# Where the tiles lie in on-chip memory: the order of the regions reversed in a two-block transformer kernel

## The chip, the cores and the metric

The kernel runs on one core of one Trainium2 chip. The metric is the time of one execution on the device, in microseconds. Before the change it was 2476.69 us, the median of 3 runs (2471.95 to 2477.06).

A core has TensorE (PE in the profile), which multiplies: it holds a 128x128 *stationary* operand and streams a *moving* operand of up to 512 columns past it, and the result goes to one of 8 banks of PSUM. VectorE (DVE), ScalarE (ACT) and GpSimd (POOL) work on tiles elementwise; SyncE (SP) issues the transfers from HBM. The on-chip memory (SBUF) has 128 partitions; a tile takes the same range of bytes in each, and "address" below means the first byte of a tile in a partition.

## The reference, cut to what matters

A sequence of 512 tokens of width 1024 goes through two blocks (the lines above the loop, and the loop), all in float32:

```
x = x + 0.5 * rms_norm(swiglu_ffn(rms_norm(x)))            # up0, down0: 1024 -> 2*2816 -> 1024
x = x + rms_norm(token_mixer(rms_norm(x)))                 # mixin, hgrn2 and mLSTM, mixout
x = x + 0.5 * rms_norm(swiglu_ffn(rms_norm(x)))            # up1, down1
for layer in range(2):
    mix = mixer_ab(x) if layer == 0 else mixer_c(x)        # ab, about; cin, cout
    x = layer_norm(alpha * x + mix)
    x = layer_norm(alpha * x + cross_attend(x, mem))       # kv, q, wo; mem has 256 rows
    x = layer_norm(alpha * x + conv_ffn(x))                # up2, down2; up3, down3
```

Most of the arithmetic is products of activations with weight matrices. Each such product is done in three matmuls: a float32 matrix W is split into W_hi (rounded to the format float32r that TensorE takes at one column per step) and W_lo = W - W_hi, the activations likewise, and W_hi*A_hi + W_lo*A_hi + W_hi*A_lo is accumulated.

## The kernel before, in words

**Work and queues.** The weights come as 208 pieces of 1 MB, called units, in the order of use. SP transfers each into one of four slots (`raw`, 8 KB of a partition each). ACT copies `raw` to `w_hi` (line 935), DVE computes `w_lo` = `raw` - `w_hi` in the place of `raw` (line 1322), and PE uses the unit in 48 or 96 matmuls. Each engine has one program written by hand, with semaphores between them; the order of the work is fixed in these programs. PE's is the sequence at the end of its block: `head_units`, `feature_units`, `down`, `token_units`, `mix_out`, `attention` and so on for each stage in `PHASES`.

**Who is stationary and who moves.** In `mm(out, A, B)` A is the stationary operand, 128 columns, and B is the moving one. The profile names the moving operand first: `bank<-a_hi,w_hi` streams a_hi past a stationary w_hi.

- `feature_tile` (line 420): weights stationary, activations `a_hi`, `a_lo` moving, 512 columns, or 256 in `head_units`. Used in up, mixin, ab, cin and q. Line 704 is the same inside the mixer's core.
- `token_tile` (line 459): activations stationary, weights moving, 256 columns.
- `rows_part` (line 494): activations stationary, weights moving, 512 columns. The activations are `h_hi`, `h_lo` in the down projections, `a_hi`, `a_lo` in mixout and about, `y_hi`, `y_lo` in cout (about and cout both through `mix_out`), and `o_hi`, `o_lo` in the attention's output projection wo.
- `mlstm_rows` (line 587): `wg_hi`, `wg_lo` stationary, `a_hi`, `a_lo` moving, 512 columns.
- `memory_unit` (line 745), 256 columns: in the first four units of kv0 and kv1 the weights are stationary and `mem_hi`, `mem_lo` move; in the last four it is the other way round.

**Where the tiles lie.** One slab of 228160 bytes a partition starts at address BASE = 1152. Every tile is placed in it by a byte offset (`at`, line 68). Before the change the order from the lowest address is: `x` (16 KB), `a_hi`, `a_lo` (16 KB each), the slots `raw` = `w_lo` (32 KB) and `w_hi` (32 KB), then 3904 bytes of constants (`ident`, `ones`, `vec`, `small`, `stat`, `bnl`, `tri`), then the arena. In addresses: x 1152, a_hi 17536, a_lo 33920, w_lo 50304, w_hi 83072 to 115840, constants 115840 to 119744, arena from 119744. `row0`, used at the start only, lies in w_hi's place.

The arena (`arena`, line 92) is shared by stages that follow each other; a stage's tiles overlay those of others, at offsets given in KB of the arena. In it are h_hi (at 0), h_lo (44 KB), y_hi (24 KB), y_lo (40 KB), o_hi (48 KB), o_lo (64 KB), mem_hi (64 KB), mem_lo (72 KB), wg_hi (68 KB), wg_lo (72 KB), and all small tiles of the mixers and of the attention. Its last tile ends at 106.5 KB.

Of the kernel before, what the change touches and what calls it, by code (L numbers as in the profile page):

```python
# [4 lines left out]
P = 128  # L5
T = 512
D = 1024
KD = D // P
# [3 lines left out]
NT = T // P  # L12
HEADS = 4
CHUNK = 128
FULL = 16 * P
LEVELS = (64, 32, 16, 8, 4, 2, 1)
ALPHA = (2 * 2) ** 0.25
SLOTS = 4
# [38 lines left out]
def build(nc, a):  # L57
    f32, f32r, u32 = mybir.dt.float32, mybir.dt.float32r, mybir.dt.uint32
# [4 lines left out]
    with ctx:  # L63
        KB = 1024
        BASE = 1152
        slab = ctx.enter_context(nc.sbuf_tensor("slab", [P, 57040], f32))

        def at(name, shape, dt, off):
            return nc.alloc_sbuf_tensor_at(name, shape, dt, offset=BASE + int(off))

        x = at("x", [P, NT, D], f32, 0)
        a_hi = at("a_hi", [P, KD, T], f32r, 16 * KB)
        a_lo = at("a_lo", [P, KD, T], f32r, 32 * KB)

        raw = at("raw", [P, SLOTS, FULL], f32, 48 * KB)
        w_lo = at("w_lo", [P, SLOTS, FULL], f32r, 48 * KB)
        w_hi = at("w_hi", [P, SLOTS, FULL], f32r, 80 * KB)
        C0 = 112 * KB
        ident = at("ident", [P, P], f32, C0)
        ones = at("ones", [P, P], f32, C0 + 512)  # L80
        vec = at("vec", [P, N_VEC], f32, C0 + 1024)
        C1 = C0 + 1024 + (N_VEC * 4 + 31) // 32 * 32
        small = at("small", [P, 8], f32, C1)
        eps6, eps5, one, primed, eps24 = (small[:, n:n + 1] for n in range(5))
        stat = at("stat", [P, NT, 8], f32, C1 + 32)
        row0 = at("row0", [1, D], f32, 80 * KB)
        bnl = at("bnl", [P, NT, 12], f32, C1 + 160)
        tri = at("tri", [P, 2, P], f32, C1 + 352)
        A0 = C0 + 3904

        def arena(name, shape, dt, kb):
            return at(name, shape, dt, A0 + kb * KB)

# [1810 lines left out]
```

## Time and profile before

| | |
|---|---|
| three runs | 2471.95, 2477.06, 2476.69 us; median 2476.69 |
| the profiled execution | 2474.66 us, span 2472.9 us, mean granted clock 0.989 |
| PE | busy 2436.9 us (99%), 12340 matmuls |
| PE weight loads | busy 2054.3 us (83%), beside the matmuls |
| DVE, ACT, POOL | busy 1112.6, 801.2, 63.6 us |
| transfers | 238.31 MB, mean 96 GB/s; q1 busy 27.1% of the 16 engines' span |

How to read it: the span is from the first instruction to the last of one profiled execution. Busy time of PE is a union of intervals whose ends are modelled: a matmul of 512 columns is drawn with some 390 ns, and the next starts before that. The pace of PE is therefore the distance between starts. The chain of waits (the chain of work that ended last) helps: where it runs along PE, a piece of it is the time from the first start to the last of a run of matmuls of one line, with their count.

### The profile page before, as it was taken

Reading aid. Unit: us, or ns where it says so; the run is one execution under the profiler, and the core shown is the slowest. Engines: PE = TensorE matmul, PEld = TensorE weight load, DVE = VectorE, ACT = ScalarE, POOL = GpSimd, SP = SyncE. Lnnn points to the kernel's source line nnn. Section 1 sums busy time; section 2 is a strip of 40 time slices with the busy share of each in tenths; the row PEclk is TensorE's granted clock in tenths of the full one; section 3 lists DMA queues with packets and bytes.
Section 4 is the critical chain, followed back from the end, with each engine's and each line's share of the span. In section 5 each row is a group of like instructions: output and inputs, shape, how many; then the busy total and the mean of one; then the engine's idle time right before and its main releaser. Section 6 shows DMA issues by size and latency. Waiting matters only on the chain.

```text
span 2472.9 us, 27382 instructions
## 1 busy us (share of the span) xinstructions
PE 2436.9 (99%) x12340; PEld 2054.3 (83%) x12340; DVE 1112.6 (45%) x1054; ACT 801.2 (32%) x879; POOL 63.6 (3%) x38
## 2 busy tenths in 40 slices
PE   9999999998999999999999999999999999999998
PEld 8888889886888888888887888888888977888886
DVE  4333226534753333147634644432634635544424
ACT  4222225343442222133343333321322332433311
POOL 0000000002300000000001000000000000000000
PEclk9999999997999999999999999999999999999999
DMA  4222323210112332233331322222332421222321
GB/s 159 101 87 102 112 75 114 85 67 18 52 69 103 103 102 94 102 114 113 120 136 34 120 85 102 103 102 85 120 119 85 177 79 64 90 102 85 119 94 60
DMA packets 34406, 238.31 MB, mean 96 GB/s; under 512 B 3949, under 2 KB 4333, under 8 KB 6514
## 3 DMA queue, kind: packets, MB, share of 16 engines
q1 hardware_dynamic: 34288, 236.56, 27.1%
q8 instruction: 97, 1.59, 0.3%
q14 instruction: 19, 0.16, 0.0%
q10 hardware_dynamic: 2, 0.00, 0.0%
HBM read 234.46 MB, written 2.10 MB: 96 GB/s over the span
## 4 chain that ended last, share of the span: by engine, by line
PE 96%; DVE 2%; ACT 1%; issue 0%; DMA 0%; DVEq 0%; ACTq 0%
PE bank L420 52%; PE bank L494 29%; PE bank L459 4%; PE bank L745 4%; PE bank L482 1%; PE bank L772 1%; PE bank L671 1%; PE bank L792 1%; PE bank L704 1%; PE bank L626 0%; PE bank L631 0%; PE bank L617 0%; PE bank L654 0%; PE bank L587 0%; PE bank L647 0%
## 5 line engine op out<-in xcount | busy, mean ns | idle before, releaser
L420 PE MATMUL bank<-a_hi,w_hi 128*128 128x512 f32 (+1 forms) x2112 | 778.2, 368 | 0.6 <-DVE a_lo L1371 0.6
L420 PE MATMUL bank<-a_lo,w_hi 128*128 128x512 f32 (+1 forms) x2112 | 774.7, 367 | 0.0
L420 PE MATMUL bank<-a_hi,w_lo 128*128 128x512 f32 (+1 forms) x2112 | 774.7, 367 | 0.0
L1322 DVE TENSOR_TENSOR w_lo<-raw,w_hi 128x2048 fp32r<-128x2048 f32 x207 | 474.0, 2291 | 513.7 <-ACT w_hi L935 513.1
L935 ACT ACTIVATE w_hi<-raw 128x2048 fp32r<-128x2048 f32 x207 | 394.4, 1906 | 357.0 <-DMA raw<-w_full 357.0
L420 PEld LDWEIGHTS bank<-a_hi,w_hi 128*128 128x128 f32 x2112 | 398.5, 189 | 66.9 <-DVE a_lo L1371 0.8
L420 PEld LDWEIGHTS bank<-a_lo,w_hi 128*128 128x128 f32 x2112 | 398.5, 189 | 65.6
L420 PEld LDWEIGHTS bank<-a_hi,w_lo 128*128 128x128 f32 x2112 | 398.6, 189 | 65.2 <-issue 0.5
L494 PE MATMUL bank<-w_hi,h_hi 128*128 128x512 f32 x704 | 278.9, 396 | 0.0
L494 PE MATMUL bank<-w_hi,h_lo 128*128 128x512 f32 x704 | 278.4, 395 | 0.0
L494 PE MATMUL bank<-w_lo,h_hi 128*128 128x512 f32 x704 | 278.3, 395 | 0.0
L1391 DVE TENSOR_TENSOR h<-act_out,bank 128x512 f32<-128x512 f32 x88 | 60.5, 687 | 353.4 <-PE bank L420 350.6
L984 ACT ACTIVATE h_hi<-h 128x512 fp32r<-128x512 f32 x88 | 55.6, 632 | 367.0 <-DVE h L1391 367.0
L494 PEld LDWEIGHTS bank<-w_hi,h_lo 128*128 128x128 f32 x704 | 132.3, 188 | 32.0
L494 PEld LDWEIGHTS bank<-w_lo,h_hi 128*128 128x128 f32 x704 | 132.3, 188 | 31.7
L494 PEld LDWEIGHTS bank<-w_hi,h_hi 128*128 128x128 f32 x704 | 132.3, 188 | 31.6
L1393 DVE TENSOR_TENSOR h_lo<-h,h_hi 128x512 fp32r<-128x512 f32 x88 | 61.0, 693 | 61.4 <-ACT h_hi L984 61.4
L1384 DVE SCALAR_TENSOR_TENSOR conv_out<-bank,vec,conv_out 128x511 f32<-128x511 f32 x88 | 65.9, 749 | 36.5 <-ACT conv_out L976 34.9
L459 PE MATMUL bank<-w_hi,a_hi 128*128 128x256 f32 x256 | 74.3, 290 | 0.0
L459 PE MATMUL bank<-w_lo,a_hi 128*128 128x256 f32 x256 | 73.7, 288 | 0.0
L459 PE MATMUL bank<-w_hi,a_lo 128*128 128x256 f32 x256 | 73.5, 287 | 0.0
L976 ACT ACTIVATE conv_out<-bank,vec 128x512 f32<-128x512 f32 x44 | 34.2, 777 | 94.0 <-PE bank L420 94.0
(283 smaller groups left out, 2424.3 us busy)
## 6 DMA issues: line engine op xcount, KB each, us to landing
raw<-w_full SPq DMA_DIRECT2D x207, 1024.0 KB, 4.7
rows_ab<-rows SPq DMA_DIRECT2D x8, 1024.0 KB, 5.5
x<-x SPq DMA_DIRECT2D x4, 512.0 KB, 6.7
mem_raw<-mem SPq DMA_DIRECT2D x2, 1024.0 KB, 8.0
out<-x SPq DMA_DIRECT2D x4, 512.0 KB, 2.6
raw<-w_full SPq DMA_DIRECT2D x2, 512.0 KB, 7.3
ab_rows<-ab_rows SPq DMA_DIRECT2D x1, 768.0 KB, 6.3
wg_raw<-w_gates SPq DMA_DIRECT2D x1, 512.0 KB, 5.7
```

What stands on the lines that cost most here:

```text
L420: last = mm(bank[:, b + m, cols], w[:, s, c0:c0 + P], act_in[:, k, cols], start=(k == 0 and j == 0), stop=(k == KD - 1 and j == 2))
L459: last = mm(bank[:, b, c0:c0 + 256], act_in[:, k, tok(t)], w[:, s, k * 256:k * 256 + 256], start=(k == 0 and j == 0), stop=(k == KD - 1 an ...
L482: last = nc.tensor.transpose(pair(b)[:, k, :], src[:, row, k * P:(k + 1) * P], ident[:, :])
L494: done = mm(bank[:, 2 * t + n, :], act_in[:, k, tok(t)], w[:, s, c0:c0 + T], start=(first and r == 0 and j == 0), stop=(last and r == 1 an ...
L745: last = mm(bank[:, b + m, 0:MEM], *ops, start=(k == 0 and j == 0), stop=(k == KD - 1 and j == 2))
L935: S.activation(w_hi[:, u % SLOTS, :], raw[:, u % SLOTS, :], ACT.Copy).then_inc(w_hi_done, 1)
L976: S.activation(conv_out[:, s, :], bank[:, b, :], ACT.Identity, scale=vec[:, vc + 2 * KF + n:vc + 2 * KF + n + 1], bias=vec[:, vb + n:vb + ...
L984: S.activation(h_hi[:, n, :], h32[:, s, :], ACT.Copy).then_inc(h_hi_done, 1)
L1322: V.tensor_tensor(w_lo[:, u % SLOTS, :], raw[:, u % SLOTS, :], w_hi[:, u % SLOTS, :], ALU.subtract).then_inc(w_split, 1)
L1384: V.scalar_tensor_tensor(conv_out[:, s, tap:T], bank[:, b, 0:T - tap], vec[:, vc + (2 - tap) * KF + n:vc + (2 - tap) * KF + n + 1], conv_o ...
L1391: V.tensor_tensor(h32[:, s, :], act_out[:, s, :], bank[:, b + 1, :], ALU.mult).then_inc(ffn_banks, 1)
L1393: V.tensor_tensor(h_lo[:, n, :], h32[:, s, :], h_hi[:, n, :], ALU.subtract).then_inc(h_done, 1)
```

## The change

The arena gets the lowest addresses, and x with everything that followed it comes behind the arena. Nothing else is edited: all tiles keep their sizes, the arena's tiles keep their offsets in the arena, and x, a_hi, a_lo, the slots and the constants keep their distances from each other. The instructions of every engine and their order are the same as before; each line of the code behind the edit has a number higher by one.

```
+        X0 = 107 * KB - 512
-        x = at("x", [P, NT, D], f32, 0)
-        a_hi = at("a_hi", [P, KD, T], f32r, 16 * KB)
-        a_lo = at("a_lo", [P, KD, T], f32r, 32 * KB)
-        raw = at("raw", [P, SLOTS, FULL], f32, 48 * KB)
-        w_lo = at("w_lo", [P, SLOTS, FULL], f32r, 48 * KB)
-        w_hi = at("w_hi", [P, SLOTS, FULL], f32r, 80 * KB)
-        C0 = 112 * KB
+        x = at("x", [P, NT, D], f32, X0)
+        a_hi = at("a_hi", [P, KD, T], f32r, X0 + 16 * KB)
+        a_lo = at("a_lo", [P, KD, T], f32r, X0 + 32 * KB)
+        raw = at("raw", [P, SLOTS, FULL], f32, X0 + 48 * KB)
+        w_lo = at("w_lo", [P, SLOTS, FULL], f32r, X0 + 48 * KB)
+        w_hi = at("w_hi", [P, SLOTS, FULL], f32r, X0 + 80 * KB)
+        C0 = X0 + 112 * KB
...
-        row0 = at("row0", [1, D], f32, 80 * KB)
+        row0 = at("row0", [1, D], f32, X0 + 80 * KB)
...
-        A0 = C0 + 3904
+        A0 = 0
```

In addresses, after: arena from 1152 to 110208, x 110208, a_hi 126592, a_lo 142976, w_lo 159360, w_hi 192128 to 224896, constants from 224896.

## Rows read from the trace of the kernel before

**Rows 1.** The page: span, busy PE, chain that ended last by engine

```profile
span 2472.9 us, 27382 instructions
...
PE 2436.9 (99%) x12340; PEld 2054.3 (83%) x12340; DVE 1112.6 (45%) x1054; ACT 801.2 (32%) x879; POOL 63.6 (3%) x38
...
PE 96%; DVE 2%; ACT 1%; issue 0%; DMA 0%; DVEq 0%; ACTq 0%
```

**Rows 2.** Chain of waits, longest pieces: start us, us, what, matmuls

```profile
261.23 109.20 PE bank L494 x468
...
1167.83 43.56 PE bank L494 x192
...
1883.16 44.80 PE bank L494 x192
```

**Rows 3.** Chain of waits from 410 to 442 us

```profile
412.34 5.60 PE bank L587 x24
417.94 23.02 PE bank L459 x192
```

**Rows 4.** Chain of waits from 1210 to 1276 us

```profile
1211.39 5.66 PE bank L745 x48
...
1237.51 21.78 PE bank L745 x192
1259.29 16.34 PE bank L420 x72
```

**Rows 5.** Chain of waits from 1340 to 1394 us

```profile
1343.74 25.21 PE bank L494 x108
```

**Rows 6.** PE by line and shape: xcount, busy us, mean ns, idle before

```profile
L420 PE MATMUL bank<-a_hi,w_hi 128*128 128x512 f32 x1664 | 650.0, 391 | 0.0
...
L494 PE MATMUL bank<-w_hi,h_hi 128*128 128x512 f32 x704 | 278.9, 396 | 0.0
...
L420 PE MATMUL bank<-a_hi,w_hi 128*128 128x256 f32 x448 | 128.2, 286 | 0.6 <-DVE a_lo L1371 0.6
...
L459 PE MATMUL bank<-w_hi,a_hi 128*128 128x256 f32 x256 | 74.3, 290 | 0.0
...
L494 PE MATMUL bank<-w_hi,o_hi 128*128 128x512 f32 x128 | 52.8, 412 | 2.2 <-DVE o L1791 2.2
L494 PE MATMUL bank<-w_hi,a_hi 128*128 128x512 f32 x128 | 51.2, 400 | 0.5 <-DVE a_lo L1452 0.5
...
L745 PE MATMUL bank<-mem_hi,w_hi 128*128 128x256 f32 x128 | 36.2, 283 | 0.0
...
L745 PE MATMUL bank<-w_hi,mem_hi 128*128 128x256 f32 x128 | 35.5, 277 | 0.0
...
L494 PE MATMUL bank<-w_hi,y_hi 128*128 128x512 f32 x64 | 25.3, 396 | 0.0
...
L587 PE MATMUL bank<-a_hi,wg_hi 128*128 128x512 f32 x8 | 3.2, 396 | 0.0
```

**Rows 7.** PE in order of time, 107.3 to 108.8 us: start, us, instruction

```profile
107.39 0.39 PE L420 MATMUL bank<-a_hi,w_hi 128*128 128x512 f32 x1
...
108.75 0.39 PE L420 MATMUL bank<-a_hi,w_hi 128*128 128x512 f32 x1
```

**Rows 8.** DVE and ACT by line and shape, columns as in rows 6

```profile
L1322 DVE TENSOR_TENSOR w_lo<-raw,w_hi 128x2048 fp32r<-128x2048 f32 x207 | 474.0, 2291 | 513.7 <-ACT w_hi L935 513.1
...
L1709 DVE TENSOR_TENSOR mem_lo<-mem_raw,mem_hi 128x2048 fp32r<-128x2048 f32 x1 | 2.3, 2283 | 0.0
...
L935 ACT ACTIVATE w_hi<-raw 128x2048 fp32r<-128x2048 f32 x207 | 394.4, 1906 | 357.0 <-DMA raw<-w_full 357.0
...
L1204 ACT ACTIVATE mem_hi<-mem_raw 128x2048 fp32r<-128x2048 f32 x1 | 1.9, 1902 | 0.0
```

**Rows 9.** Busy time from 480 to 700 us, with the granted clock (PEclk)

```profile
480.00:700.00 220.00, 201.26 (x1191) 172.99 (x1191) 118.97 (x141) 88.42 (x115) 38.83 (x18) 0.90 0.13 46
```

**Rows 10.** Longest waits of PE; transfers of weight units on the page

```profile
PE bank L494 <- DVE o L1791: 2.2, 2, 1.1
...
raw<-w_full SPq DMA_DIRECT2D x207, 1024.0 KB, 4.7
```

## The prediction

> **What bounds the kernel now.** I read the page first: TensorE is busy in 2436.9 of the 2472.9 us, and the chain of work that ended last lies on PE for 96% of the span [rows 1]. No other engine holds the end for more than 2%. So a change pays only if it changes how fast PE gets through its 12340 matmuls, or how long it waits. The change adds, removes and reorders no instruction: every engine's list is the same before and after, only the addresses differ. What is left is to ask whether a matmul's pace depends on where its operands lie.
>
> For that the mean duration of a matmul is of little use. It is about 390 to 396 ns for all forms with 512 columns [rows 6], while the next one starts much earlier; the ends are modelled. The pace has to be read as length divided by count, from pieces of the chain of waits that hold one line only, in an undisturbed stretch.
>
> - L494 in the first down projection, weights (w_hi, w_lo) streaming, stationary operand h_hi or h_lo: 109.20 us for 468 matmuls, 233.3 ns each [rows 2].
> - L494 in "about", the same line, the same order, the same streaming operand, stationary a_hi or a_lo: 43.56 us for 192, 226.9 ns [rows 2].
> - L494 in "cout", written by the same function mix_out as "about", stationary y_hi or y_lo: 44.80 us for 192, 233.3 ns [rows 2].
> - L494 in the attention's output projection, stationary o_hi or o_lo: 25.21 us for 108, 233.4 ns [rows 5].
> - L587, roles turned: a_hi and a_lo stream, wg_hi and wg_lo are stationary: 5.60 us for 24, 233.3 ns [rows 3].
> - L420, a_hi and a_lo stream, w_hi and w_lo stationary: 16.34 us for 72, 226.9 ns [rows 4].
>
> So there are two paces at full clock, 226.9 and 233.3 ns, 6.45 ns apart, and the slow one goes with a stationary operand in the arena, whichever tile is streamed. With 256 columns the arena shows too, with the other sign: 119.9 ns where neither operand is in it (L459, 23.02 us for 192) [rows 3]; 117.9 ns where the memory (mem_hi, mem_lo) streams from it (5.66 us for 48), and 113.4 ns where it is the stationary operand (21.78 us for 192) [rows 4].
>
> **What the arena has that the others have not.** Two things, and the code gives both. In bytes of a partition, x starts at 1152, and x, a_hi, a_lo, w_lo and w_hi all start at 128 past a multiple of 512. The arena starts at 1152 + 112*1024 + 3904 = 119744: that is 64 past a multiple of 128 (448 past a multiple of 512), and it is above all the other big tiles. The 3904 bytes of constants did that. So either the odd remainder sets the pace (remainder theory) or the height does (position theory). From one matmul to the next the addresses step by 512 or 2048 bytes with k and m, and the pace stays within each piece: multiples of 512 don't seem to matter.
>
> Position needs a border between 115840, where w_hi ends, and 119744. The highest stationary tiles of w_hi, in slot 3 (at 114816 and 115328 bytes), are read by the last six matmuls of the unit that ends at 108.75 us: from 107.39 to 108.75 are six steps of 227 ns, the fast pace, though they lie above the middle of the 228160 bytes in use [rows 7]. A border just there would be odd; a remainder fits with no border at all. I take the remainder for the likelier by far.
>
> **The change part by part.** The arena goes to offset 0, so it starts at 1152 = 9*128. x goes to 107*1024 - 512 = 109056 past the base, 110208 = 861*128, and a_hi, a_lo, the slots and the constants keep their distances from x. Now every big tile, arena included, is 128 past a multiple of 512. That is the pair of remainders that L420 and L494 in "about" have today.
>
> 1. L494 with a stationary operand in the arena: h 3 x 704 = 2112, o 3 x 128 = 384, y 3 x 64 = 192, and L587 3 x 8 = 24 [rows 6]; together 2712 matmuls. Each goes from 233.3 to 226.9: 2712 x 6.45 ns = 17.5 us less.
> 2. L745, memory streaming: 384 matmuls [rows 6] go from 117.9 to 119.9: 0.8 us more. L745, memory stationary: 384 from 113.4 to 119.9: 2.5 us more. Together 3.3 us.
> 3. L420 and L459 and L494 with a_hi: remainders as before, nothing.
> 4. ACT and DVE: no sign that place matters. DVE's 128x2048 subtraction takes 2291 ns for w_lo, outside the arena, and 2283 for mem_lo, in it; ACT's copy 1906 ns for w_hi and 1902 for mem_hi [rows 8]. Nothing.
> 5. What could swallow the gain: in the down projections a unit of 48 matmuls will take 10.89 us instead of 11.20, and needs a transfer of 4.7 us and the splits of 1.91 and 2.29 us [rows 8, 10]. The up projections already live on 10.89 us a unit without waiting. Nothing new becomes late. In the woven output projection PE waits 2.2 us in all for DVE's copy of o [rows 10]; at worst that takes back the 384 x 6.45 = 2.5 us of o.
>
> Sum: 17.5 - 3.3 = 14.2 us less. The profiled execution took 2474.66 us (span 2472.9 and 1.8 around it), so 2460.5 us by it. The three runs had a median of 2476.69, within 2471.95 to 2477.06; I forecast from the median: 2476.7 - 14.2 = 2462.5 us, 0.57% less.
>
> Bounds for this case: if item 2 doesn't come, 17.5 less, 2459.2; if o gains nothing, 11.7 less, 2465.0. Between 480 and 700 us the granted clock is 0.90 of full, with PE busy for 201.26 of the 220 us [rows 9], so parts of it run at the lower of the two levels (1.2 instead of 2.4 GHz); the first down projection ends 3.4 us earlier than now (528 x 6.45 ns), so those stretches fall on other matmuls, worth about 3 us either way. With the spread of the runs this gives 2456 to 2469.
>
> **The Trainium skill.** The rows show that one and the same instruction has two paces. The page "SBUF — State Buffer" of the Trainium skill, section "Who interferes with whom", says that PE has two independent read ports and never waits on anyone. By that rule a change of addresses does nothing and the time stays at 2476.7, the first rival; the trace has a difference of 6.45 ns by tile that it doesn't explain. Its section "Operand start alignment" says of element-aligned addresses that they are legal and that nothing was timed, so it takes no side.
>
> **The rivals.**
> - No change, 2476.7 us. The pace would hang on the relation between the two operands' places, for instance fast where both lie below the border or both above, slow where they lie apart. After the change a and w are both above, h, o, y and wg are still apart from what streams beside them: every pair keeps its pace. For it: all slow pairs of today are apart. Against it: the border in an odd place, and that apart is faster at 256 columns and slower at 512.
> - Slower, 2490 us. Position theory: whatever is stationary above the border costs 6.45 ns at 512 columns. Then the 17.5 us of item 1 are won, but L420 (3 x 1664) and L494 with a_hi (3 x 128), 5376 matmuls [rows 6], now fetch from above: 34.7 us more. L745 with the memory stationary, now below, gives back 2.5. At 256 columns L420 (3 x 448) and L459 (3 x 256), 2112 matmuls, would go between 0 and 119.9 - 113.4 = 6.5 ns faster, 0 to 13.7 us. Net 6.0 to 19.7 us more, middle 13: 2483 to 2496. It decides from 17.5 us / 5376 = 3.3 ns for each of those matmuls. Against it: rows 7, and that an address bit for such a border doesn't exist between 115840 and 119744.
> - The gain comes but doesn't reach the end, since waits take its place: in the down projections nothing speaks for it (item 5), and 2465 is its mild form.
>
> **How the numbers follow.** Remainder theory 0.76, no change 0.11, slower by position 0.12, and 0.01 for a gain too small to tell. About 0.2%, 5 us, is what a measurement of this kernel can tell from no change. So faster 0.77, within 0.2% 0.11, slower 0.12. The range for 8 in 10: the likeliest case alone has 2456 to 2469 and holds about 7 in 10, so it must reach over the case of no change with its spread: 2456 to 2478.
>
> **What would show it.** Right: in the chain of waits the piece of L494 x468 of the first down projection falls from 109.20 to about 106.2 us, "cout" from 44.80 to 43.56 for x192, L587 from 5.60 to 5.44, while L745 x192 rises from 21.78 to about 23.0 and L745 x48 from 5.66 to 5.75. "about" stays at 43.56 and L420 x72 at 16.34. Wrong, position: L420 x72 at 16.8 and "about" at 44.80. Wrong, relation: all pieces as they are. If all pieces move as said but the end doesn't, a wait took the gain, and the waits of PE in the mixer between 480 and 700 us are the place to look.

## The result and the profile after

The changed kernel takes 2457.6 us, the median of 4 runs (2457.16 to 2459.61), against 2476.27 us before (4 runs, 2471.95 to 2477.06): a ratio of 0.9932, 95% interval 0.992 to 0.9945. It is 0.7% faster, 18.7 us, where 14.2 us had been forecast. The profiled execution took 2457.16 us.

From the page of the profile after, the lines that answer to [rows 1]:

```profile
span 2455.4 us, 27382 instructions
...
PE 2416.6 (98%) x12340; PEld 2052.9 (84%) x12340; DVE 1113.9 (45%) x1054; ACT 801.0 (33%) x879; POOL 63.6 (3%) x38
```

As many instructions as before, DVE and ACT as busy as before; PE is busy for 20.3 us less. The chain of waits after, with start, length, line and count; L495, L588, L746 and L421 are the old L494, L587, L745 and L420:

```profile
261.02 106.09 PE bank L495 x468
...
1157.59 43.54 PE bank L495 x192
...
1869.92 43.52 PE bank L495 x192
```

```profile
408.62 5.47 PE bank L588 x24
414.09 23.03 PE bank L460 x192
...
1201.13 5.75 PE bank L746 x48
...
1227.62 23.03 PE bank L746 x192
1250.64 16.35 PE bank L421 x72
...
1334.99 24.50 PE bank L495 x108
```

Against [rows 2 to 5]: the first down projection has 106.09 us in place of 109.20, cout 43.52 in place of 44.80, L588 5.47 in place of 5.60, the attention's output projection 24.50 in place of 25.21. The memory projections are slower as forecast, 23.03 in place of 21.78 and 5.75 in place of 5.66. About, L460 and L421 stand still (43.54, 23.03, 16.35). So outside the mixer the pieces of 512 columns now have a pace of 226.7 to 226.9 ns, and those of 256 columns one of 119.8 to 120.0. L588 has 227.9 in the mean: its first five distances between starts are 229 to 236 ns and the other nineteen 226 or 227, while before all 24 were 230 to 236.

Summed over all distances between starts of matmuls of a line and tile in the two traces, L495 with h gives 13.9 us, with o 2.3, with y 1.3, L588 0.1, and the memory projections take 3.2 back: 14.4 us. The span is 17.5 us shorter. Of the other 3.1 us, 2.9 lie in one place, the token mixer, and 0.2 at the start of the kernel. Busy time from 480 to 700 us after, to compare with [rows 9]:

```profile
480.00:700.00 220.00, 198.49 (x1195) 170.80 (x1195) 119.19 (x138) 87.47 (x117) 38.81 (x18) 0.93 0.13 46
```

The granted clock was 0.93 there in this execution and 0.90 in the one of before; PE did about as many matmuls (1195 and 1191) in 198.49 us of busy time as in 201.26. Whether that belongs to the change is taken up below.

### The profile page after: what moved, and what is told of

It reads as the page before. It is cut to its first block, busy times and chain, and to the rows that moved or that the text cites. A ratio compares the mean times of both kernels' runs of the same rounds, so it can differ in the third digit from the quotient of the medians.

```text
span 2455.4 us, 27382 instructions
## 1 busy us (share of the span) xinstructions
PE 2416.6 (98%) x12340; PEld 2052.9 (84%) x12340; DVE 1113.9 (45%) x1054; ACT 801.0 (33%) x879; POOL 63.6 (3%) x38
## 4 chain that ended last, share of the span: by engine, by line
PE 96%; DVE 2%; ACT 1%; issue 0%; POOL 0%; DMA 0%; DVEq 0%; POOLq 0%; ACTq 0%
PE bank L421 52%; PE bank L495 28%; PE bank L460 4%; PE bank L746 4%; PE bank L483 1%; PE bank L773 1%; PE bank L672 1%; PE bank L793 1%; PE bank L705 1%; DVE w_lo L1323 0%; PE bank L627 0%; PE bank L632 0%; PE bank L618 0%; PE bank L648 0%; PE bank L588 0%
## 5 line engine op out<-in xcount | busy, mean ns | idle before, releaser
L421 PE MATMUL bank<-a_hi,w_hi 128*128 128x512 f32 (+1 forms) x2112 | 777.4, 368 | 0.6 <-DVE a_lo L1372 0.6
L421 PE MATMUL bank<-a_hi,w_lo 128*128 128x512 f32 (+1 forms) x2112 | 774.1, 367 | 0.0
L421 PE MATMUL bank<-a_lo,w_hi 128*128 128x512 f32 (+1 forms) x2112 | 774.1, 367 | 0.0
L421 PEld LDWEIGHTS bank<-a_hi,w_hi 128*128 128x128 f32 x2112 | 398.2, 189 | 67.1 <-DVE a_lo L1372 0.8
L421 PEld LDWEIGHTS bank<-a_lo,w_hi 128*128 128x128 f32 x2112 | 398.2, 189 | 65.1
L421 PEld LDWEIGHTS bank<-a_hi,w_lo 128*128 128x128 f32 x2112 | 398.3, 189 | 64.9 <-issue 0.5
L495 PE MATMUL bank<-w_hi,h_hi 128*128 128x512 f32 x704 | 274.4, 390 | 0.0
L495 PE MATMUL bank<-w_hi,h_lo 128*128 128x512 f32 x704 | 273.9, 389 | 0.0
L495 PE MATMUL bank<-w_lo,h_hi 128*128 128x512 f32 x704 | 273.9, 389 | 0.0
L495 PEld LDWEIGHTS bank<-w_hi,h_lo 128*128 128x128 f32 x704 | 132.1, 188 | 27.6
L495 PEld LDWEIGHTS bank<-w_hi,h_hi 128*128 128x128 f32 x704 | 132.1, 188 | 27.2
L495 PEld LDWEIGHTS bank<-w_lo,h_hi 128*128 128x128 f32 x704 | 132.2, 188 | 27.2
L460 PE MATMUL bank<-w_hi,a_hi 128*128 128x256 f32 x256 | 74.3, 290 | 0.0
L460 PE MATMUL bank<-w_lo,a_hi 128*128 128x256 f32 x256 | 73.7, 288 | 0.0
L460 PE MATMUL bank<-w_hi,a_lo 128*128 128x256 f32 x256 | 73.6, 288 | 0.0
```

Source lines behind the costliest of these rows:

```text
L421: last = mm(bank[:, b + m, cols], w[:, s, c0:c0 + P], act_in[:, k, cols], start=(k == 0 and j == 0), stop=(k == KD - 1 and j == 2))
L460: last = mm(bank[:, b, c0:c0 + 256], act_in[:, k, tok(t)], w[:, s, k * 256:k * 256 + 256], start=(k == 0 and j == 0), stop=(k == KD - 1 an ...
L495: done = mm(bank[:, 2 * t + n, :], act_in[:, k, tok(t)], w[:, s, c0:c0 + T], start=(first and r == 0 and j == 0), stop=(last and r == 1 an ...
```

## The experiments

The question after this result: the paces came as forecast, but is the reason the remainder of the stationary operand's own address, its height, or its distance from the streamed operand? Each ratio is to the kernel before, run on the same chip. The pace is again the length of a piece of the chain of waits by its count. The *difference* below is the stationary operand's address minus the moving one's.

**e1_arena_up_64.** The old order, arena on a multiple of 512.

```
-        A0 = C0 + 3904
+        A0 = C0 + 3968
```

> The old order of the regions, with the arena 64 bytes higher, at 119808: a multiple of 512, and still above all other big tiles. Remainder theory (a stationary operand 64 past a multiple of 128 costs 6.45 ns at 512 columns): as fast as the changed kernel, the piece of L494 x468 falls from 109.20 to 106.1 us, cout x192 from 44.80 to 43.5, L587 x24 from 5.60 to 5.5, and the kv pieces rise, L745 x192 from 21.78 to 23.0; in all 14.2 us less than before, near 2460. Position theory (height costs): nothing changes, 2476, since the arena is as high as it was. If the remainder of 512 must be the same as that of the streamed operand (128), not only that of 128: nothing changes either.

Measured: 2475.3 us, ratio 1.0 (0.9991 to 1.001). The chain of waits of this run:

```profile
261.80 108.75 PE bank L494 x468
...
1168.61 43.55 PE bank L494 x192
...
1884.77 44.63 PE bank L494 x192
```

The stationary operand is on a multiple of 512 and the pace is 232.4 ns, nearly the slow one. The remainder theory, the one on which I had put 0.76, is wrong as stated: a clean address alone buys 0.9 of the 6.6 ns, and nothing that the time shows.

**e2_low_arena_off_64.** The new order, arena at 1216.

```
-        X0 = 107 * KB - 512
+        X0 = 107 * KB
...
-        A0 = 0
+        A0 = 64
```

> The new order of the regions, the arena at the bottom but 64 bytes past a multiple of 128 (at 1216), and x and what follows it 512 bytes higher, so at the same remainder as in the changed kernel. Remainder theory: all that the change won is lost, L495 x468 is 109.2 us again, cout x192 44.8, L746 x192 21.8; 2457.6 + 14.2 = about 2472, up to 2476. Position theory, or the order of the regions as such: stays at 2457.6.

Measured: 2473.15 us, ratio 1.0 (0.999 to 1.0009).

```profile
261.61 109.20 PE bank L495 x468
...
1165.25 43.56 PE bank L495 x192
...
1880.55 44.80 PE bank L495 x192
```

To a hundredth of a microsecond the lengths are those of before [rows 2], with the arena at the bottom. Height and order of the regions are out.

**e3_rest_off_64.** The new order, the arena at 1152, everything else 64 bytes up.

```
-        X0 = 107 * KB - 512
+        X0 = 107 * KB - 448
```

> The new order, the arena at 1152 as in the changed kernel, but x, a_hi, a_lo, the weight slots and the constants 64 bytes higher, so 64 past a multiple of 128. It gives a moving operand off the multiple at 512 columns (L495 with h, y, o, and L588), which no trace has shown yet. If only the stationary operand's own remainder counts: L421 x72 goes from 16.35 to 16.8 us, the piece of L495 in about from 43.54 to 44.8, while L495 x468 with h stays at 106.1; 5376 matmuls x 6.45 = 34.7 us more; at 256 columns 2112 matmuls with a stationary weight or activation tile off gain between 0 and 6.5 ns, 0 to 13.7 us, and kv 3.3: 2475 to 2489. If the difference between the two operands' remainders counts, not the stationary one's own: L421 stays at 16.35, about at 43.54, and L495 x468 with h goes to 109.2: 2472 to 2476.

Measured: 2459.52 us, ratio 0.9936 (0.9921 to 0.9951).

```profile
261.04 107.13 PE bank L495 x468
...
1158.32 43.56 PE bank L495 x192
```

```profile
1227.80 22.61 PE bank L746 x192
1250.41 16.33 PE bank L421 x72
```

Here a and w are both 64 past a multiple of 128, and L421 (16.33) and about (43.56) keep the fast pace. Only the pairs with one operand in the arena changed: 228.9 ns for h, 117.8 for L746. What counts is the difference between the two operands. The expectation had taken the difference -64 to be as bad as 64; it is not (107.13 us, not 109.2), and so the time lies below both ranges that had been expected.

**e4_all_off_64.** The new order, everything 64 bytes up.

```
+        X0 = 107 * KB - 448
...
+        A0 = 64
```

> The new order with everything, arena included, 64 bytes higher: every big tile 64 past a multiple of 128, all distances as in the changed kernel. If the stationary operand's own remainder counts: all 8088 matmuls of 512 columns in two-part arithmetic go to 233.3 ns, 52.2 us more, less what the 2880 matmuls of 256 columns gain (0 to 6.5 ns each, 0 to 18.7 us): 2491 to 2510. If only the difference between the operands counts: 2457.6, every pace as in the changed kernel.

Measured: 2460.68 us, ratio 0.9941 (0.9925 to 0.9958).

```profile
260.75 106.08 PE bank L495 x468
...
1159.97 43.53 PE bank L495 x192
...
1872.31 43.52 PE bank L495 x192
```

Every big tile has the remainder that I had blamed, and these paces are those of the changed kernel. With e1 this settles it against the operand's own remainder. The time is 3.1 us above the changed kernel's first median; the part on the size below comes back to this.

**e5_old_order_diff_0.** The old order, arena at a difference of 464 x 256 bytes from x.

```
-        A0 = C0 + 3904
+        A0 = C0 + 4096
```

> The old order of the regions, the arena 192 bytes higher (119936), so that stationary and streamed operands differ by a multiple of 256 bytes (118784 = 464 x 256) as in the changed kernel. Difference theory (the pace depends on the difference of the two operands' addresses modulo 256; 0 gives 226.7 ns, 64 gives 233.3, 128 gives 232.4, 192 gives 228.9): every pace as in the changed kernel, L494 x468 106.1 us, L745 x192 23.0, time 2457 to 2460, and the order of the regions is worth nothing. Order theory (the arena must be low, or the weights high): 2474.

Measured: 2461.83 us (2459.36 to 2462.41), ratio 0.9945 (0.9932 to 0.9959).

```profile
261.73 106.09 PE bank L494 x468
...
731.75 232.05 PE bank L420 x1080
...
1162.00 43.53 PE bank L494 x192
...
1874.33 43.52 PE bank L494 x192
```

```profile
1232.03 23.03 PE bank L745 x192
1255.05 16.35 PE bank L420 x72
```

All these paces are those of the changed kernel, with the regions in the old order, by one number. The reversal itself changes no pace; what it did was to make the arena's distance from the rest a multiple of 256. The time is 4.2 us above the changed kernel's first median and misses the upper end of what was expected by 1.8.

**p1_diffs_32_96_160_224 and p2_diffs_16_48_192_240.** The new order with own h tiles for each of the four down projections. The edit of p1, without its other lines; h_lo is placed alike, and the memory tiles are 32 bytes up in p1 and 224 in p2:

```
-        h_hi = arena("h_hi", [P, KF, T], f32r, 0)
+        def off(name, kb, d):
+            t = arena(name, [P, KF * T + 4], f32r, kb + d // 32 * 32 / KB)
+            return t[:, d % 32 // 4:d % 32 // 4 + KF * T].rearrange("p (k t) -> p k t", t=T)
+        h_hi = [off(f"h_hi{f}", 0, d) for f, d in enumerate((32, 96, 160, 224))]
```

> The new order; each of the four down projections has its own h_hi and h_lo, 32, 96, 160 and 224 bytes higher than in the changed kernel, and mem_hi, mem_lo, k_mem are 32 higher; act_out, h32, conv_out, rows_ab and ln_u 256 higher to make room. One L495 pace each for four differences. Smooth theory: between the neighbours that are known, so 32: about 230, 96: about 233, 160: about 230.5, 224: about 228. Block theory (only the 64-byte block in which an operand starts counts): 32 as 0 or as 64, that is 226.7 or 233.3, and so on. With mem 32 higher the stationary one in kv between 113.4 and 119.9 ns, smooth 116.7.

> As the last, with 16, 48, 192 and 240 bytes for the four down projections and 224 for mem_hi, mem_lo, k_mem. 192 must repeat the 228.9 ns that the kernel with x and the rest 64 bytes higher showed, in another way of getting there; otherwise the difference modulo 256 is not the whole of it. Smooth theory: 16 about 228, 48 about 232, 240 about 227. Block theory: 16 and 48 alike.

Measured: 2474.22 us (ratio 0.9994, 0.9984 to 1.0004) and 2465.02 us (0.9957, 0.9943 to 0.9972). The four down projections of p1, then of p2, in order of time:

```profile
260.82 109.19 PE bank L499 x468
...
965.32 109.64 PE bank L499 x468
...
1623.75 109.20 PE bank L499 x468
...
2338.68 123.21 PE bank L499 x528
```

```profile
262.01 106.09 PE bank L499 x468
...
964.43 109.20 PE bank L499 x468
...
1622.30 107.12 PE bank L499 x468
...
2334.85 119.69 PE bank L499 x528
```

So 32, 96, 160 and 224 bytes give 233.3, 234.3, 233.3 and 233.4 ns; 16, 48, 192 and 240 give 226.7, 233.3, 228.9 and 226.7. The value for 192 repeats that of e3. Smooth theory fails (32 is as bad as 64, and 224 is worse than 192), and block theory too (16 is free, 48 is not).

The memory projections of the same runs give two more differences at 256 columns, and each of them twice. Stationary, the memory has the difference 32 in p1 (22.72 us for 192 matmuls, 118.3 ns) and 224 in p2 (22.41, 116.7); streaming, it has 224 in p1 (5.61 us for 48, 116.9) and 32 in p2 (5.68, 118.3). The 118.3 for the stationary one in p1 is not the 116.7 of the smooth theory.

**s1_one_of_three.** As p1, with the pairs (h_hi, h_lo) at (0, 64), (64, 256), (8, 8) and (248, 248), and the memory tiles where the changed kernel has them. Of the three matmuls of a product, two have h_hi as the stationary operand and one has h_lo.

```
+        h_hi = [off(f"h_hi{f}", 0, d) for f, d in enumerate((0, 64, 8, 248))]
+        h_lo = [off(f"h_lo{f}", 44, d) for f, d in enumerate((64, 256, 8, 248))]
```

> Which matmul of the three of a split product pays. First down projection: h_hi at difference 0, h_lo at 64, so one stationary operand of three is off. Second: h_hi at 64, h_lo at 0, two of three. Third: both 8 bytes up; fourth: both 248, that is 8 down. If each matmul pays for its own difference: 226.7 + 2.2 = 228.9 ns in the mean of the first, 231.1 of the second. If the pace is one locked pattern: 226.7 or 233.3 in either. Third between 226.7 and the 227.4 of 16 bytes; fourth 226.7, as 240.

Measured, one run: 2472.75 us.

```profile
261.06 108.15 PE bank L499 x468
...
965.87 109.20 PE bank L499 x468
...
1624.67 107.95 PE bank L499 x468
...
2339.06 123.22 PE bank L499 x528
```

One of three off: 231.1 ns; two of three off: 233.3. Neither theory held: one stationary operand in three costs two thirds of the full price (4.4 of 6.6 ns), not a third, and two cost all of it. The distances between starts in this trace say where: from the start of the matmul with h_lo at 64 to the next start it is 236 ns, after the two others 228 and 229. In the kernel before, where all three are at 64, the distances alternate between 231 and 236; in the changed kernel they are 226 and 227. The eight-byte steps are slow as well (230.7 for 8, 233.4 for 248) where 16 and 240 are free.

**b1_mem_up_64.** The changed kernel with the memory tiles at 64.

```
+        mem_hi = arena("mem_hi", [P, KD, MEM], f32r, 64 + 64 / KB)
+        mem_lo = arena("mem_lo", [P, KD, MEM], f32r, 72 + 64 / KB)
+        k_mem = arena("k_mem", [P, KD, MEM], f32, 80 + 64 / KB)
```

> The changed kernel with mem_hi, mem_lo and k_mem 64 bytes higher (and rows_ab and ln_u 256), so that the 256-column matmuls of kv get back what they had before: 113.4 ns with the memory stationary, 117.8 with it streaming. Difference theory: L746 x192 from 23.03 to 21.8 us and each L746 x48 from 5.75 to 5.66, 3.2 us less than the changed kernel's 2457.6, so about 2454.4. If PE's time in kv is not on the path: no change.

Measured: 2456.77 us (2456.27 to 2459.21), ratio 0.9928 (0.9915 to 0.9942).

```profile
1205.08 5.66 PE bank L746 x48
...
1231.21 21.78 PE bank L746 x192
1252.99 16.34 PE bank L421 x72
```

The paces came back exactly. The time did not tell: 0.8 us below the changed kernel's first median, and the intervals overlap. Between the two profiled executions 3.2 us were won in kv and 3.9 lost by the end of the mixer, where no operand had moved. That kv's time is on the path is shown; that the whole kernel gained by it is not.

**c1_all_256_at_diff_64, with a2_changed_again beside it.** Every stage of 256 columns at a difference of 64.

```
+PITCH = FULL + 64
...
+def shift(g):
+    name = max((n for n, _ in PHASES if U0[n] <= g), key=U0.get)
+    u = g - U0[name]
+    if name[:2] == "kv":
+        return 16 if u < 4 else 48
+    if name[:2] == "up" or name in ("mixin", "ab", "cin"):
+        if u < 2:
+            return 16
+        if (name, u) in TOKENS:
+            return 48
+    return 0
+def unit(t, g, first=0, last=FULL):
+    return t[:, g % SLOTS, shift(g) + first:shift(g) + last]
```

Transfers, splits and matmuls address a unit's slot by it; 16 and 48 elements are 64 and 192 bytes, the latter for units that stream, whose difference is then -192, that is 64. The slots are 8448 bytes apart in place of 8192. The tile `sel` moves to make room, and ACT issues its transfer.

> The changed kernel with every stage whose matmuls have 256 columns at a difference of 64 bytes instead of 0, and all others left at 0: weight slots get a pitch 256 bytes wider, and a unit is put 64 bytes into its slot for the first two units of up, mixin, ab and cin and the first four of kv, 192 bytes for the token-major units and the last four of kv (sel moves to make room, and ACT issues its transfer). 2880 matmuls of 256 columns. Difference theory: each goes from 119.9 ns to between 117.8 (the pace that such pieces showed when entered behind the transposes) and 113.4: 6.0 to 18.7 us less than the changed kernel, 2439 to 2452, L460 x192 from 23.03 to 21.8. If the shifts cost the transfers or the splits something: L422-like pieces with waits for w_lo.

> The changed kernel itself once more, on the same chip as the others of this call, so that they can be compared with it: 2457 to 2460.

Measured: 2451.57 us (2450.38 to 2452.85), ratio to before 0.9903 (0.989 to 0.9917), against 2459.54 us (2457.08 to 2459.99), 0.9933 (0.992 to 0.9947), of the changed kernel beside it. This version beats both kernels: 8.0 us below the changed one and 24.5 below the one before, and its runs overlap with neither's. Chain of waits of c1 (L446 is the old L420, L485 the old L459, L772 the old L745), and of a2:

```profile
29.23 231.76 PE bank L446 x1080
260.99 106.08 PE bank L520 x468
413.39 22.61 PE bank L485 x192
```

```profile
1199.41 5.66 PE bank L772 x48
...
1225.53 21.78 PE bank L772 x192
```

```profile
29.23 232.03 PE bank L421 x1080
261.25 106.08 PE bank L495 x468
414.37 23.03 PE bank L460 x192
```

The 256-column matmuls ran at 117.8 ns in this piece of L485 and at 113.4 in L772 x192, at the same difference (for the first the expectation had 21.8 us, 113.5 ns). Most stretches took one of the two paces and kept it; in two pieces of L446 it went from 117.8 to 113.4 behind a single longer distance of 208 or 209 ns. Summed as above, L446 with 256 columns gives 4.0 us, L485 3.6 and L772 3.2, together 10.8. The two profiled executions are only 6.5 us apart: between 526 and 725 us of a2, in the mixer and mixout, c1 lost 3.4 us again. Its granted clock from 480 to 700 us was 0.89, that of a2 0.93.

## Why the prediction was right, and where its reason was wrong

The time, 2457.6, lies in the range and 4.9 us below the forecast.

1. *PE's pace is the bound and is to be read as length by count.* Right. Outside the mixer nothing but paces changed, to within 0.2 us.
2. *2712 matmuls gain 6.45 ns, 17.5 us.* Right: 17.6 by the sum over the traces. The last fraction comes since the fast pace of L495 with h is 226.7, not the 226.9 of about.
3. *kv gives back 0.8 + 2.5 us.* Right: 3.2.
4. *Items 3 to 5, nothing else.* Right outside the mixer: PE's wait for o is 2.2 us after as before, and no stage began to wait for weights. At the start of mixout one wait of 1.4 us for w_lo appeared, which the kernel before doesn't have. It is no mark of the change: e2, with the paces of before, has one of 1.2 us, and e5, with those of the changed kernel, has none.
5. *The remainder theory.* Wrong, and this is the step that failed: "either the odd remainder sets the pace (remainder theory) or the height does (position theory)". The remainder of the one operand doesn't matter (e1, e4), the height neither (e2, e5). It is the difference of the two operands' addresses modulo 256. Before, it was 64 where the stationary operand was in the arena, 192 where the moving one was (kv's first units), and 0 for the other split products; the change made it 0 everywhere. The period is not 512: before has 320 modulo 512 and e2 has 64, and both give 233.3 ns; e3 has 448 and p2 192, and both give 228.9. c1, half of whose slots lie an odd multiple of 256 away from h, is fast all the same (106.08 us). It is not 128 either, since 64 and 192 differ. The forecast came out since its last sentence on the layout, that all tiles now have the remainders that the fast pairs have today, holds for the difference as well. In this the forecast had luck: any reason by which the arena's pairs become like the others gave the same 14.2 us, and the wrong one gave it too. The trace of before could not tell the two apart, but it held a hint that I passed over: the memory in kv, at one and the same remainder, had two prices (113.4 stationary and 117.9 streaming). Their differences are 64 and 192. At 256 columns that is not the whole of it, as c1 has both prices at 64.
6. *The rival "no change" by relation.* It had the right kind of cause, the relation of the two places, with the wrong relation (same side of a border). The slower rival had nothing: no pace went up with the address. One argument against it was wrong, though: an address bit for a border is there, as 118784, a multiple of 4096, lies between 115840 and 119744. The rival fails by e2 and e5.
7. *The size, 4.5 us beyond the forecast.* Of the 18.7 us, 14.4 are paces. The rest, about 3 us in the profiled execution, lies in the mixer and goes with its granted clock, which I had put at 3 us either way. It is not a fixed part of the change: the changed kernel itself, run again as a2, was 16.5 us faster than before, and e5, with the same paces, 14.1. The busy time of e5 from 480 to 700 us, and that of a2:

```profile
480.00:700.00 220.00, 201.28 (x1170) 172.15 (x1169) 116.79 (x136) 86.76 (x114) 38.79 (x18) 0.88 0.13 46
```

```profile
480.00:700.00 220.00, 198.52 (x1196) 170.96 (x1195) 119.04 (x138) 87.75 (x117) 38.81 (x18) 0.93 0.13 46
```

   In the changed kernel the second long piece of L421 starts at 727.33 us, in e5 that of L420 at 731.75, and after that the two run alike. Runs of equal clock show the same: with a mean granted clock of 0.992 or 0.993 over the whole execution, the kernel before took 2471.5 to 2472.1 us (six runs) and the changed one 2457.1 to 2457.6 (three). Their means are 14.5 us apart, about the sum of the paces. So the two medians differ by more because the executions drew different clocks: 0.991 or more in 8 of 44 of the kernel before, in 5 of 9 of the changed one. The paces of before don't prevent it, since e2 drew that in 5 of 10; e5 did in none of 4 and e4 in one of 4. What decides it, and whether the layout has a part in it, is open: the runs of the changed kernel and of e5 (2457.1 to 2460.0 and 2459.4 to 2462.4) hardly overlap, and no run here was made to explain it.

On the rule that PE never waits on anyone: no run here was made to test it against another engine's accesses. What the runs show is that a matmul's pace depends on the addresses of its own two operands. The Trainium skill's page "SBUF — State Buffer", section "Who interferes with whom", counts two independent read ports for PE, and taken as "addresses don't matter" it would have missed 14.4 us here.

## What to carry to other kernels

When the same matmul runs at two paces in one trace, compare the addresses of its two operands before anything else. In this kernel, 512-column matmuls were fastest where the tiles that meet as stationary and moving operand were a multiple of 256 bytes apart (16 and 240 bytes more were as fast, all other differences tried were slower); 3904 bytes of constants in front of a region were enough to spoil that. Then look at the shapes one by one, since with 256 columns other differences were the better ones. And to separate two explanations that coincide in a layout, shift one region, then the other, then both.

## What the runs showed of the hardware

All for float32r operands of 128 partitions at the full granted clock, the stationary operand changed with every matmul; the difference is the stationary operand's address minus the moving one's, modulo 256 bytes. The values are means over a piece.

| difference | 512 columns, ns | seen in | 256 columns, ns | seen in |
|---|---|---|---|---|
| 0 | 226.7 | after, e4, e5 | 119.9 | after, e5 |
| 8 | 230.7 | s1 | | |
| 16 | 226.7 | p2 | | |
| 32 | 233.3 | p1 | 118.3 | p1, p2 |
| 48 | 233.3 | p2 | | |
| 64 | 233.3 | before, e2 | 113.4, or 117.8 | before, b1, c1, e3 |
| 96 | 234.3 | p1 | | |
| 128 | 232.4 | e1 | 118.6, or 120.0 | e1 |
| 160 | 233.3 | p1 | | |
| 192 | 228.9 | e3, p2 | 117.8 | before, b1, e3 |
| 224 | 233.4 | p1 | 116.7 to 116.9 | p1, p2 |
| 240 | 226.7 | p2 | | |
| 248 | 233.4 | s1 | | |

With 512 columns it made no difference which of the tiles was activations or weights, nor whether both were high, both low or apart. At 256 columns the streaming memory had 117.8 ns in c1 where the stationary one had 113.4, both at 64.

No run here shows a mechanism. The loads of stationary operands run beside the matmuls (busy 84% of the span after), so the operand that matters could be that of the matmul itself or the next one, which is loaded meanwhile; except in s1 the two have the same remainder, and s1 doesn't decide it. That the numbers are not monotone, that slow distances alternate between 231 and 236 ns, and that a stretch can keep either of two paces at the same difference would fit a pattern in time between the load and the stream. That is a guess and was not tested.
